# Attention units of a one-core network kernel: exponentials left unnormalised, value products once per branch, gates applied over the sums afterwards

## What is computed

```
s   = q k^T - slope(head) * distance          # per head, causal
p   = exp(s - max s) / sum exp(s - max s)     # masked softmax
o_c = p_c @ v_cmp        # compressed branch: 31 compressed positions
o_s = p_s @ v_s          # selected branch: with 512 positions all 8 blocks are selected, so it is causal attention
o_w = p_w @ v_w          # window branch: the window is 512, so it is causal attention too
o   = (gate0 * o_c + gate1 * o_s + gate2 * o_w) * silu(z)
y   = o @ w_out
```

## Time and profile before

| | |
|---|---|
| median of 3 runs | 1366.69 us (1363.32 to 1366.7) |
| profiled execution, device time | 1361.53 us |
| its span, first to last instruction | 1359.7 us |
| busy PE / DVE / ACT / POOL | 94% / 58% / 32% / 61% of the span |
| mean granted TensorE clock | 0.985 of 2.4 GHz |
| attention units, first score product to first product of the output projection | 858.84 us to 1027.02 us of the span |

### The profile page before, as it was taken

One profiled execution on the slowest core, in us unless ns is written; L12 is line 12 of the kernel. 1 busy time (PEld: TensorE's weight loads), 2 busy tenths in 40 slices (PEclk: granted clock), 3 DMA queues, 4 the chain that ended last, 5 costly groups with the idle time before them and its releaser, 6 DMA issues.

```text
span 1359.7 us, 22827 instructions
## 1 busy us (share of the span) xinstructions
PE 1282.3 (94%) x8112; PEld 1019.5 (75%) x8112; DVE 790.4 (58%) x1214; ACT 434.3 (32%) x866; POOL 834.2 (61%) x1062
## 2 busy tenths in 40 slices
PE   6999998999999999999989999899999998999986
PEld 4778996878877888888768797555557786878874
DVE  5978665589798111796327353487783568722223
ACT  4165734243200233112200121777772201231111
POOL 7767623778999777998657628100005773567762
PEclk9999999999999999999999999899999998999998
DMA  5222101243326433346582303000006359423321
GB/s 192 79 76 78 49 3 31 83 135 98 93 74 205 155 98 95 109 132 178 199 260 85 85 19 98 9 1 1 1 1 230 106 143 265 172 77 93 100 78 69
DMA packets 86478, 137.93 MB, mean 101 GB/s; under 512 B 16512, under 2 KB 34432, under 8 KB 85376
## 3 DMA queue, kind: packets, MB, share of 16 engines
q1 hardware_dynamic: 48384, 88.10, 22.2%
q10 hardware_dynamic: 38016, 48.71, 11.2%
HBM read 119.02 MB, written 20.91 MB: 103 GB/s over the span
## 4 chain that ended last, share of the span: by engine, by line
PE 77%; DVE 8%; issue 4%; POOL 3%; ACTq 3%; ACT 2%; DMA 2%; POOLq 0%; DVEq 0%
PE ps L386 19%; PE ps L388 18%; PE ps L387 18%; PE ps L777 3%; PE ps L788 3%; PE ps L800 3%; PE ps L529 2%; ACTq L1166 2%; POOL small L1399 1%; DVE acc L1489 1%; PE ps L681 1%; PE ps L726 1%; PE ps L857 1%; DMA bigB<-lags_scratch 1%; POOL wh L1400 1%
## 5 line engine op out<-in xcount | busy, mean ns | idle before, releaser
L1402 POOL TENSOR_TENSOR wl<-raw,wh 128x512 fp32r<-128x512 f32 x336 | 497.5, 1481 | 26.9
L1399 POOL TENSOR_TENSOR small<-small 1x1 f32<-1x1 f32 x336 | 118.2, 352 | 330.6 <-PE ps L388 325.4
L386 PE MATMUL ps<-uH,wh 128*128 128x512 f32 x672 | 267.3, 398 | 18.6 <-DVE uL L1479 11.5
L387 PE MATMUL ps<-uL,wh 128*128 128x512 f32 x672 | 263.3, 392 | 0.0
L388 PE MATMUL ps<-uH,wl 128*128 128x512 f32 x672 | 263.1, 392 | 0.0
L1400 POOL CAST wh<-raw 128x512 fp32r<-128x512 f32 x336 | 203.2, 605 | 0.0
L386 PEld LDWEIGHTS ps<-uH,wh 128*128 128x128 f32 x672 | 127.3, 189 | 48.4 <-issue 16.7
L387 PEld LDWEIGHTS ps<-uL,wh 128*128 128x128 f32 x672 | 127.4, 190 | 27.3 <-issue 1.4
L388 PEld LDWEIGHTS ps<-uH,wl 128*128 128x128 f32 x672 | 127.3, 189 | 26.8
L386 PE MATMUL ps<-ffH,wh 128*128 128x512 f32 x256 | 101.3, 396 | 4.4 <-POOL wl L1402 4.3
L387 PE MATMUL ps<-ffL,wh 128*128 128x512 f32 x256 | 99.8, 390 | 0.0
(11 more groups left out here) (387 smaller groups left out, 2442.1 us busy)
## 6 DMA issues: line engine op xcount, KB each, us to landing
raw<-wstream SPq DMA_DIRECT2D x336, 256.0 KB, 2.7
b_powers_scratch<-bigB ACTq DMA_DIRECT2D x4, 1024.0 KB, 5.0
c_powers_scratch<-bigB ACTq DMA_DIRECT2D x8, 512.0 KB, 4.2
lags_scratch<-lag_rows_scratch ACTq DMA_DIRECT2D x8, 512.0 KB, 9.9
bigB<-b_powers_scratch ACTq DMA_DIRECT2D x4, 1024.0 KB, 8.2
bigB<-lags_scratch ACTq DMA_DIRECT2D x4, 1024.0 KB, 8.8
bigB<-c_powers_scratch ACTq DMA_DIRECT2D x4, 1024.0 KB, 11.5
hT<-x ACTq DMA_DIRECT2D x4, 512.0 KB, 7.5
```

What stands on the lines that cost most here:

```text
L386: pe.matmul(out, lh, rh, start=first, stop=False)
L387: pe.matmul(out, lh, rl, start=False, stop=False)
L1399: pool.tensor_tensor(small[0:1, 569 + j:570 + j], zero_ap[0:1], zero_ap[0:1], ALU.add)
L1402: pool.tensor_tensor(wl[:, j, :], raw[:, j, :], wh[:, j, :].bitcast(f32), ALU.subtract).then_inc(half_split, 1)
```

## The change

The units are reordered: for each pair all four query tiles of one branch, then the four of the other (`UNITS` is now (t, b, qt)). Four units of one (t, b) are a **group**; there are 16. What happens to them:

- `weigh` is gone: the exponentials stay unnormalised. The sums of a group are inverted once (`invert`, one reciprocal of 128 x 8).
- POOL multiplies the inverted sums by the gates, spread out over 64 columns for each head (one instruction of 128 x 512 per group), PE transposes that (`spread`, 4 transposes, into bank 7), so that a 128 x 512 tile of factors lies as the values do.
- The value products are made once per group into bank 6: for key tile `kt` all query tiles from kt on, 512 - 128 kt columns in one product.
- `finish` is made once per group, in three DVE instructions that each wait for the one before: factors times silu(z), values times that, and an addition (of the compressed part for the first branch, of the first branch for the second).
- The compressed branch is made beforehand for all 8 pairs (`cmp_values`, `cmp_branch`), 512 columns a product, its probabilities already gated as before.
- The copies of the transposes of query tile 3 move from ACT to DVE (`turned`).
- `prob` has six places; a unit is turned three steps after its scores (`LAG`); `probT` has two places of a whole group.

```diff
-        prob = view(bigB, 9216, 3, 2, 512)
-        probT = view(bigB, 12288, 3, 2, 512)
+        prob = view(bigB, 9216, 6, 2, 512)
+        probT = [view(bigB, 4096 * i, 2, TT, 512) for i in range(2)]
-        UNITS = [(t, qt, b) for t in range(KT) for qt in range(TT) for b in range(2)]
+        UNITS = [(t, b, qt) for t in range(KT) for b in range(2) for qt in range(TT)]
+        NGROUP = 2 * KT
+        LAG = 3
...
+        def turned(engine, u, copy):
+            t, b, qt = UNITS[u]
+            g = 2 * t + b
+            engine.wait_ge(at_t, u + 1)
+            if qt == 0:
+                if g >= 2:
+                    engine.wait_ge(at_v, 2 * g - 3)
...
+            copy(probT[g % 2][:, :, 0:qt + 1, qt * 128:(qt + 1) * 128],
+                 ps[:, 4:6, 0:(qt + 1) * 128].rearrange("p a (k c) -> p a k c", c=128)).then_inc(at_ev, 1)
...
             def turn(u):
-                pe.wait_ge(at_p, u + 1)
+                pe.wait_ge(at_e, u + 1)
                 if u >= 1:
                     pe.wait_ge(at_ev, u)
...
+            def cmp_values(t):
+                if t >= 2:
+                    pe.wait_ge(cs_p, TT + t - 1)
+                for half in range(2):
+                    g = t // 4 * 2 + half
+                    i = pe.matmul(ps[64 * half:64 * half + 64, 6 + t % 2, :], vcmp[:, g * DH:(g + 1) * DH], pcT[:, half * 8 + t, :],
+                                  start=True, stop=True)
+                i.then_inc(cs_t, 1)
+            def values(g):
+                t, b = g // 2, g % 2
+                pe.wait_ge(at_ev, 4 * g + 4)
...
+                for kt in range(TT):
+                    for half in range(2):
+                        h = t // 4 * 2 + half
+                        i = pe.matmul(ps[64 * half:64 * half + 64, 6, kt * 128:512], vtok[:, kt, b * 256 + h * DH:b * 256 + (h + 1) * DH],
+                                      probT[g % 2][:, half, kt, kt * 128:512], start=kt == 0, stop=kt == TT - 1)
                 i.then_inc(at_v, 1)
+            def spread(g):
+                pe.wait_ge(at_x, g + 1)
...
+                for qt in range(TT):
+                    i = pe.transpose(ps[:, 7, qt * 128:(qt + 1) * 128], spread_gates[:, qt * 128:(qt + 1) * 128], ident)
+                i.then_inc(at_v, 1)
-            for n in range(len(UNITS) + 3):
+            for n in range(4 * NGROUP + LAG + 2):
                 if n < len(UNITS):
                     scores(n)
-                if 2 <= n <= len(UNITS) + 1:
-                    turn(n - 2)
-                if n >= 3:
-                    values(n - 3)
+                if n < 2:
+                    for t in range(4 * n, 4 * n + 4):
+                        cmp_values(t)
+                if LAG <= n < len(UNITS) + LAG:
+                    turn(n - LAG)
+                if n >= LAG + 4 and (n - LAG) % 4 == 0:
+                    values((n - LAG) // 4 - 1)
+                if n >= LAG + 5 and (n - LAG) % 4 == 1:
+                    spread((n - LAG) // 4 - 1)
...
+            for g in range(NGROUP):
+                t, b = g // 2, g % 2
+                if b and t + 2 < KT:
+                    slopes(t + 2)
+                pool.wait_ge(at_r, g + 1)
...
+                pool.tensor_tensor(spread_gates.rearrange("p (t a d) -> p t a d", a=2, d=DH),
+                                   rsum[:, g % 2].unsqueeze(3).to_broadcast([128, TT, 2, DH]),
+                                   gate[:, :, 1 + b, t::KT].unsqueeze(3).to_broadcast([128, TT, 2, DH]), ALU.mult).then_inc(at_x, 1)
...
+            def invert(g):
+                dve.wait_ge(at_e, 4 * g + 4)
+                dve.reciprocal(rsum[:, g % 2], asum[:, g % 2]).then_inc(at_r, 1)
+            def finish(g):
+                t, b = g // 2, g % 2
+                dve.wait_ge(at_v, 2 * g + 2)
+                dve.tensor_tensor(rz, ps[:, 7, :], zsT[:, t, :], ALU.mult).then_inc(at_g, 1)
+                dve.wait_ge(at_g, 2 * g + 1)
+                dst = branch if b else xs[:, t % 2, :]
+                dve.tensor_tensor(dst, ps[:, 6, :], rz, ALU.mult).then_inc(at_g, 1)
+                dve.wait_ge(at_g, 2 * g + 2)
+                if b:
+                    dve.tensor_tensor(xs[:, t % 2, :], xs[:, t % 2, :], branch, ALU.add).then_inc(x_full, 1)
...
-            for n in range(len(UNITS) + 1):
+            for n in range(4 * NGROUP + LAG + 3):
                 if n < len(UNITS):
                     shift(n)
...
+                if LAG <= n < len(UNITS) + LAG and UNITS[n - LAG][2] == TT - 1:
+                    turned(dve, n - LAG, lambda out, x: dve.tensor_copy(out, x))
+                if n >= 5 and n % 4 == 1 and n // 4 <= NGROUP:
+                    invert(n // 4 - 1)
+                if n >= LAG + 6 and (n - LAG) % 4 == 2:
+                    finish((n - LAG) // 4 - 1)
+                if n >= LAG + 12 and (n - LAG) % 8 == 4:
+                    finish_rest((n - LAG) // 8 - 1)
```

More of the change, by code:

```diff
@@ L272, in build @@
         ds_ready = sem("slopes_ready")
-        at_qk, at_s, at_e, at_p, at_t, at_ev, at_v, at_o = (sem(f"att_{n}") for n in
-            ("scores", "scores_read", "exp", "probs", "transposed", "probsT", "value", "out"))
+        at_qk, at_s, at_e, at_t, at_ev, at_v, at_o = (sem(f"att_{n}") for n in
+            ("scores", "scores_read", "exp", "transposed", "probsT", "value_and_gates", "out"))
+        at_r, at_x, at_g = sem("att_sums_inverted"), sem("att_gates_by_sums"), sem("att_group_read")
         s_bc = sem("ssm_bc_loaded")
@@ L787, in turn @@
                     for kt in range(qt + 1):
-                        i = pe.transpose(ps[:, 4 + half, kt * 128:(kt + 1) * 128], prob[:, u % 3, half, kt * 128:(kt + 1) * 128], ident)
+                        i = pe.transpose(ps[:, 4 + half, kt * 128:(kt + 1) * 128], prob[:, u % 6, half, kt * 128:(kt + 1) * 128], ident)
                 i.then_inc(at_t, 1)
[L791 to L797, removed]
-                    for half in range(2):
[L799 to L806, removed]
-                i.then_inc(at_v, 1)
@@ L1255, in _ @@
                                ps[0:NCMP, 4 + n % 2, :].rearrange("p (h q) -> p h q", q=128), ACT.Copy).then_inc(cs_ev, 1)
[L1256 to L1263, removed]
+            for n in range(len(UNITS) + LAG):
+                if n >= LAG and UNITS[n - LAG][2] < TT - 1:
+                    turned(act, n - LAG, lambda out, x: act.activation(out, x, ACT.Copy))
                 if n < len(UNITS):
-                    t, qt, b = UNITS[n]
+                    t, b, qt = UNITS[n]
                     W = (qt + 1) * 128
@@ L1446, in _, with slopes @@
             pool.wait_ge(cmp_act, 2)
-            for n in range(NH):
-                t, half = n // 2, n % 2
+            def slopes(t):
                 if t >= 2:
                     pool.wait_ge(at_s, 8 * (t - 1))
-                pool.tensor_scalar(dsl[t % 2][:, half, :], const("dist"), const("slope")[:, half * 8 + t:half * 8 + t + 1], 0.0,
-                                   ALU.mult, ALU.add).then_inc(ds_ready, 1)
+                for half in range(2):
+                    pool.tensor_scalar(dsl[t % 2][:, half, :], const("dist"), const("slope")[:, half * 8 + t:half * 8 + t + 1], 0.0,
+                                       ALU.mult, ALU.add).then_inc(ds_ready, 1)
+            slopes(0)
+            slopes(1)
+            for g in range(NGROUP):
[3 more added lines that the diff above has]
+                pool.wait_ge(at_r, g + 1)
+                if g:
+                    pool.wait_ge(at_v, 2 * g)
+                pool.tensor_tensor(spread_gates.rearrange("p (t a d) -> p t a d", a=2, d=DH),
+                                   rsum[:, g % 2].unsqueeze(3).to_broadcast([128, TT, 2, DH]),
+                                   gate[:, :, 1 + b, t::KT].unsqueeze(3).to_broadcast([128, TT, 2, DH]), ALU.mult).then_inc(at_x, 1)
             split_weights(2 * SLOT0["nout"] + RING, 2 * NSLOT)
@@ L1978, in shift @@
                 i.then_inc(at_s, 1)
[L1980 to L1988, removed]
@@ new lines, in finish @@
+            def finish(g):
[8 more added lines that the diff above has]
+                    dve.tensor_tensor(xs[:, t % 2, :], xs[:, t % 2, :], branch, ALU.add).then_inc(x_full, 1)
+                else:
+                    dve.wait_ge(cs_p, TT + KT)
+                    own(dve.tensor_tensor(xs[:, t % 2, :], xs[:, t % 2, :], mixT[:, t, :], ALU.add))
@@ L1997, in finish_rest @@
             def finish_rest(t):
                 rest(uL[:, t, :], uH[:, t, :]).then_inc(at_o, 1)
-            for n in range(len(UNITS) + 1):
+            for n in range(4 * NGROUP + LAG + 3):
                 if n < len(UNITS):
                     shift(n)
[L2003 to L2009, removed]
+                if n < 2:
+                    for t in range(4 * n, 4 * n + 4):
+                        cmp_branch(t)
+                if LAG <= n < len(UNITS) + LAG and UNITS[n - LAG][2] == TT - 1:
[6 more added lines that the diff above has]
+                    finish_rest((n - LAG) // 8 - 1)
```

39 lines of the change are left out of this document (24 added, 15 removed).

## The result

| | before | after |
|---|---|---|
| median | 1365.14 us (1363.32 to 1366.7, 4 runs) | 1378.07 us (1375.97 to 1381.05, 4 runs) |
| span of the profiled execution | 1359.7 us | 1375.9 us |
| first score product to first product of the output projection | 168.2 us | 859.97 to 1041.69: 181.7 us |
| distance between groups in the middle | 10.17 us | 10.14 us |

The ratio is 1.0105, with an interval of 1.0085 to 1.0124: the changed kernel is slower by about 13 us (12.9 us between the medians); 10.6 us more and 1377 us were forecast. The stage grew by 13.5 us; in the same two profiled executions what stands behind it took 334.2 us against 332.7, and the stage began 1.1 us later.

What follows compares the result with a forecast made beforehand. A loop through DVE and PE was taken to bound the stage: 9.2 + 14.1 + 134.6 + 20.9 = 178.8 us against 168.2, 10.6 us more, giving 1377 us; range 1364 to 1390 us.

Steps and rivals of the forecast that it cites:

- the loop: Middle of the stage: DVE's shift, reciprocal, finish, shift and copy, then PE's turn; 10.35 us a group, 13 times.
- the ends: The stage before the tenth unit's scores and after the 62nd's: 8.2 us of the forecast growth.
- hand-over to PE: In each group, from the end of a DVE instruction to PE's start: 0.05 us.
- PE's part: PE's transposes, values, scores, transposes, gates and scores of query tile 1, up to DVE's next shift: 5.11 us a group.
- PE's share up to the wait: PE's scores 2, transposes 3 and scores 3, done about 3.7 us after query tile 1's shift starts; then waits 1.6 us.
- bound of 4.3 us for the value products: In each group's value products, if a head pair's two halves don't overlap on PE: 4.3 us instead of 2.1.
- The head: Stage start to the tenth unit's scores: first scores and compressed products 9.2 us, then 14.1 us.
- the fall: PE's clock dropping to half early in the stage: 6.4 us of work at half speed would cost some 3 us more.
- The tail: From the scores of the 62nd unit to the first product of the output projection: 20.9 us.
- DVE and POOL colliding: Rival, chance 0.10: POOL's product lengthens DVE's addition by up to 1.07 us each loop; up to 14 us, 1391 us.
- The PE-bound rival: Rival, chance 0.13: the loop isn't tight and PE sets 8.63 us a group; 13.7 us less than now, 1353 us.
- a clock that falls for good: Rival, chance 0.04: PE's waits drop the clock, about doubling its 5.1 us in each loop; +55 us, over 1420 us.

Runs made afterwards that it cites:

- the first three experiments: Against the changed kernel: query tile 3's copy back on ACT, ratio 0.9976; finish's addition moved behind that copy, 1.0029; both together, 0.9972 (ratios to the kernel before).
- the eight other variants: The eight follow-up kernels, each but the combinations one edit to the changed kernel; measured times from 1352.58 to 1377.09 us.

## Why the prediction was right, point by point

- **The cause and the size.** The mechanism held: an order that makes PE and DVE take turns in one loop, so that less work on both gives nothing. How the slowdown divides was forecast less well. Of the 10.6 us, 2.4 were to come from the loop and 8.2 from the ends (44.2 against 36.0 us); the loop gave -0.2 and the ends 13.8. And 1377 for 1378.07 us is nearer than the working deserves: the increase was forecast as 10.6 and measured as 12.9 us, and the median of the kernel before, which the forecast was put on, stood 1.5 us higher (1366.69) than the one of the result (1365.14). That part is luck.
- **The loop.** Predicted 10.35 us, measured 10.15. Its terms from the order of time above: shift 0.69 as predicted; reciprocal 0.12 for 0.16; finish 2.0 for 2.2, since its first instruction took 0.64 us, its two waits cost 0.03 and 0.04 us, and the shift behind it starts 0.08 us before it ends; shift of tile 2 0.95 for 0.97; copy 1.22 for 1.23; hand-over to PE 0.14 for 0.05; PE's part 4.94 for 5.11, with values 2.3 as predicted and the two blocks of transposes 1.02 for 1.18, because going from one to the other costs no change of kind. These sum to 10.07 us; every second group takes 10.19, since there the addition (L2049) has 0.72 us to the start of the shift behind it and not 0.61. 13 loops were 132.0 us, 2.6 us less than the 134.6 forecast. That this is a loop and not a sum of loads is shown by the first three experiments. Two readings in the working were off without harm to it. The row behind the hand-over of 0.05 us shows no wait: in the trace before, PE's scores (L777) begin at 931.72 us and take 1.13, so PE was busy until the transposes began at 932.84. And PE's share up to the wait adds up to 0.80 + 0.85 + 1.02 + 1.06 - 0.2 = 3.5 us, not 3.7; measured are 3.77 us and a wait of 1.36.
- **The bound of 4.3 us for the value products** (halves one after the other) didn't happen: 2.3 us, so halves of 512 columns do run beside one another.
- **The head.** Forecast 9.2 + 14.1 = 23.3 us, measured 28.8 (859.97 to 888.79). This is the step that was mis-sized: I counted full clock, since PE would be dense, and allowed 3 us for the fall. The compressed products took 13.6 us with the first scores instead of 9.2, and the first steps behind them, still at half clock for 3 us, 15.2 instead of 14.1. The premise that dense products keep the clock was wrong for these products; with 128 rows it held, and there the terms come out: 8.5 us to the third scores for 9.2, 14.2 from there to the tenth unit for 14.1. So the whole miss of the head is the clock, whose fall was priced at 3 us and cost 6.1.
- **The tail.** Forecast 20.9 us, measured 20.94 (1020.75 to 1041.69).
- **The sum.** 28.8 + 132.0 + 20.9 = 181.7 us, forecast 178.8. Of the 2.9 us missed, the head is +5.5 and the loop -2.6; they partly cancelled.
- **DVE and POOL colliding** was a rival with 0.10. POOL's product takes 1.04 us, against the 1.3 to 1.5 I took from other two-input instructions, which are subtractions, and is over at 942.4 us, before the last instruction of finish begins at 942.60. The additions take 0.69 us on average (L2046 and L2049). The mechanism is not refuted, it had no overlap to act on; the loop was not made to bring one about.
- **The PE-bound rival** named the right prize and the wrong kernel: 8.63 us a group is what PE has, and 8.86 is what the kernel gets once the copy is on ACT.
- **The clock in the loop** stayed full; it is at the two ends that it fell. The price that I gave for a clock that falls for good was too low: 5.1 us in each of 13 loops are 66 us, not 55. At the end PE idles for 3.6 us before the output projection, against 2.2 before, since finish for the last group stands bare with three instructions. The clock falls in that time, and the projection starts at 1.2 GHz and stays there until 1047.1 us, for 5.4 us of its work:

```profile
1039.00:1040.00 1.00, 0.00 (x0) 1.00 0.00 0
1040.00:1041.00 1.00, 0.00 (x0) 0.65 0.00 0
...
1042.00:1043.00 1.00, 1.00 (x3) 0.50 0.00 0
1046.00:1047.00 1.00, 1.00 (x4) 0.50 1.00 361
1047.00:1048.00 1.00, 1.00 (x6) 0.94 0.96 303
```

I had not counted that. 5.4 us of dense work at half clock cost 2.7 us if nothing hides it; what stands behind the stage was 1.5 us longer. These 1.5 us are near what two executions differ by. All the eight other variants have the same idle time, 3.6 or 3.7 us, and a half clock in it or soon after it, for 3.4 to 6.8 us; what stands behind their stage took 333.2 to 336.6 us, and the times don't follow the length of the half clock (6.8 us of it and 334.2 us in the changed kernel, 3.4 and 335.5 with the added zero rows). No experiment shortened that idle time, so how much of the 13 us it holds stays open.

## What to carry to other kernels

Three engines that have 6.6 to 8.6 us of work each for a period of 10 are not bound by load: write down the loop that begins and ends at one instruction and passes through every program's order, and ask of each instruction in it whether the next engine needs it yet. Less work on the engine in the loop doesn't help if what is left stands ahead of what another engine waits for; here three instructions nobody waited for stood ahead of a copy that PE did. Work taken out of a pipelined loop to be done beforehand must be charged at its full time, and at the clock that it gets there. Here the loop came out no longer than before, and these charges at the ends made the change a loss.

## What the runs showed of the hardware that was not expected

- PE busy 100% of the time and at half clock for 13.7 us with products of 31 rows by 64 columns, 512 columns streamed; with 128 rows, zeros or data, and the same columns streamed, the clock did not fall. The Trainium skill, TensorE: Matmul & The Clock Gate, Part 1, section "What's actually happening", says that the clock is set by how busy PE has been recently. If busy is read as the profile's busy time, this trace does not agree: from 863 to 876 us PE was busy for all of each microsecond and stayed at half clock. The added 97 rows of zeros cost no time of their own: in the first 1.9 us, where both kernels run at full clock, the weight loads of the compressed products start at the same distances (0, 0.49, 0.91 and 1.87 us). Why the rows matter is not shown. The first fall, at 861.7 us before and 862.8 after, came some 3 us into the stage in both kernels; that it didn't come with 128 rows is measured (in three kernels), which part of the first 3 us decides it isn't taken apart.
- A GpSimd product of two inputs that are both spread out from small tiles (128 x 512 from 128 x 8) took 1.04 us; its subtractions of two whole 128 x 512 tiles took 1.48 us on average, 1.30 in the median and 1.26 at the least.
